# An early first projection and value products paired by heads in a two-layer decoder step

## The reference, cut to what matters

```python
def dilated_group(q, k, v, q_idx, window, dil, table):
    offs = dil * jnp.arange(n_keys, dtype=jnp.int32)
    kg = k[:, idx]; vg = v[:, idx]
    bias = table.astype(jnp.float32)[rel_bucket(offs)].T
    logits = jnp.einsum('bqhd,bqjhd->bqhj', q, kg).astype(jnp.float32) * ATTN_SCALE + bias
    ...
    e = jnp.exp(logits - m)
    s = jnp.sum(e, axis=-1, keepdims=True)
    o = jnp.einsum('bqhj,bqjhd->bqhd', (e / s).astype(v.dtype), vg)
    return o, m + jnp.log(s)

def mixer_a_prompt(h, w_in, w_out, table):
    qkv = (h @ w_in).reshape(bsz, seq, N_DIL, 3, N_HEADS, HEAD_DIM)
```

## Time and profile before

| | us |
|---|---|
| median of 3 runs | 1675.91 |
| lowest and highest | 1675.38, 1677.29 |
| the profiled execution | 1680.73 |
| its span, first to last instruction | 1679.0 |
| TensorE busy | 1579.3 (94% of the span) |
| VectorE busy | 663.4 (40%) |
| ScalarE busy | 387.4 (23%) |
| GpSimd busy | 203.4 (12%) |
| start, to the first projection tile | 56.57 |
| attention A, 382.6 to 507.3 | 124.7 |
| attention B, 1131.2 to 1241.4 | 110.2 |

### The profile page before, as it was taken

How to read it: one execution, slowest core, us unless ns; L and a number is a source line. 1 busy time by engine, 2 the same in 40 slices (tenths; PEclk the granted TensorE clock), 3 DMA queues, 4 the chain that set the end, 5 groups by cost and what they waited for, 6 DMA issues and landing times.

```text
span 1679.0 us, 23479 instructions
## 1 busy us (share of the span) xinstructions
PE 1579.3 (94%) x8609; PEld 1279.6 (76%) x8609; DVE 663.4 (40%) x1533; ACT 387.4 (23%) x1166; POOL 203.4 (12%) x301
## 2 busy tenths in 40 slices
PE   6999998999989999999999999999997778999998
PEld 5877787766878878887888887886764446888886
DVE  2246512118872321003576674326546552322001
ACT  1011111113431000002566663115533220000000
POOL 1100000012230200001111120005532320000000
PEclk8799999999999999999999999999989898999999
DMA  5499999999959998787799991419966877998740
GB/s 183 158 356 383 410 401 360 337 373 355 330 164 249 284 363 299 272 292 135 128 140 140 149 186 38 122 61 352 343 200 220 285 266 242 386 372 304 276 146 31
DMA packets 170979, 423.34 MB, mean 252 GB/s; under 512 B 10400, under 2 KB 131560, under 8 KB 168064
## 3 DMA queue, kind: packets, MB, share of 16 engines
q1 hardware_dynamic: 147840, 344.27, 62.6%
q0 software_dynamic: 19312, 67.47, 15.1%
q10 hardware_dynamic: 3728, 10.32, 1.7%
HBM read 413.88 MB, written 192.48 MB: 361 GB/s over the span
## 4 chain that ended last, share of the span: by engine, by line
PE 82%; DMA 7%; DVE 7%; issue 2%; ACT 1%; SPq 1%; POOL 0%; ACTq 0%; DVEq 0%; POOLq 0%
PE bank L626 21%; PE bank L801 14%; PE bank L787 12%; PE bank L708 4%; PE bank L878 3%; PE bank L881 3%; PE bank L830 3%; PE bank L883 3%; DMA a_win_sample<-oT 2%; PE bank L719 2%; PE bank L663 2%; PE bank L756 1%; DMA cring<-cache_b_kv 1%; PE bank L1041 1%; DMA wring<-mlp_w_up 1%
## 5 line engine op out<-in xcount | busy, mean ns | idle before, releaser
L626 PE MATMUL bank<-hT,wring 128*128 128x264 f32 (+1 forms) x1488 | 354.0, 393 | 0.5 <-DVE area L1359 0.5
L626 PEld LDWEIGHTS bank<-hT,wring 128*128 128x128 f32 (+1 forms) x1488 | 279.2, 192 | 67.2 <-issue 8.2
L787 PE MATMUL bank<-hT,wring 128*128 128x264 f32 x1024 | 230.1, 388 | 1.9 <-DMA wring<-mlp_w_up 1.9
L801 PE MATMUL bank<-area,wring 128*128 128x264 f32 x1024 | 229.2, 386 | 2.8 <-DVE area L1312 2.8
L787 PEld LDWEIGHTS bank<-hT,wring 128*128 128x128 f32 x1024 | 195.6, 191 | 36.1 <-issue 2.3
L801 PEld LDWEIGHTS bank<-area,wring 128*128 128x128 f32 x1024 | 194.1, 190 | 37.2 <-DVE area L1310 3.6
L1689 ACT ACTIVATE turned<-xT 128x264 f32<-128x264 f32 x40 | 16.9, 423 | 548.1 <-DVE xT L1316 463.1
L1316 DVE TENSOR_TENSOR xT<-bank,xT 128x264 f32<-128x264 f32 x16 | 6.9, 432 | 224.6 <-PE bank L801 224.6
L1310 DVE SCALAR_TENSOR_TENSOR area<-bank,rv 128x264 f32 x64 | 27.7, 432 | 163.0 <-PE bank L787 162.3
L567 POOL TENSOR_SCALAR area<-ident,small 128x128 f32<-128x128 f32 x96 | 56.3, 603 | 179.4 <-DVE small L1392 179.4
L1242 DVE TENSOR_TENSOR area<-bank,rv 128x264 f32<-128x264 f32 x48 | 20.8, 432 | 106.0 <-PE bank L626 106.0
(11 more groups left out here) (325 smaller groups left out, 2330.7 us busy)
## 6 DMA issues: line engine op xcount, KB each, us to landing
a_win_sample<-cache_a_win SPq DMA_DIRECT2D x64, 2047.0 KB, 19.5
wring<-a_w_in SPq DMA_DIRECT2D x36, 1024.0 KB, 13.0
wring<-mlp_w_up SPq DMA_DIRECT2D x32, 1024.0 KB, 10.8
wring<-mlp_w_down SPq DMA_DIRECT2D x32, 1024.0 KB, 5.3
a_win_sample<-cache_a_win SPq DMA_DIRECT2D x16, 2044.0 KB, 19.0
cring<-cache_a_win POOLq DMA_DIRECT2D x24, 1024.0 KB, 11.9
cring<-cache_b_kv POOLq DMA_DIRECT2D x62, 256.0 KB, 6.3
cring<-cache_b_kv SPq DMA_DIRECT2D x50, 256.0 KB, 7.7
```

The source lines that it names most:

```text
L626: mm = pe.matmul(bk[half if bank is None else bank][0:width, 0:R], wring[:, blk % NW, c, half * P:half * P + width], rhs[:, c, :], start=( ...
L787: mm = pe.matmul(bk[half][:, 0:R], wring[:, blk % NW, c, half * P:(half + 1) * P], hT[:, c, :], start=(c == 0), stop=(c == DC - 1))
L801: mm = pe.matmul(bk[half][:, 0:R], wring[:, blk % NW, c, half * P:(half + 1) * P], upT[:, f * R:(f + 1) * R], start=(f == 0), stop=(f == F ...
```

## The change

**The start.** The identity is loaded first. TensorE waits for it and for x only, and for the gains ahead of their turning, by a semaphore of their own. Weight block 0 is issued ahead of `c_oh`, the masks and the bias table, which are now loaded into a part of `area` and no longer into `cring`; the first three loads of the old caches on GpSimd's queue wait for the turned gains and no longer for bias products. The bias products are cut into `bias_table(0)` to `bias_table(7)`, which stand behind tiles 1 to 8, and `bias_rest()` behind tile 9; they use banks 5 and 6. VectorE's copies of them stand between its copies of the tiles in the same way.

**Both prompt attentions.** `unit(u)` gives head 2(u // 4) + u % 2 and qt = (u // 2) % 2: two heads of the same half follow each other, so two narrow units are followed by two wide ones. `score_banks(u)` lets the scores go through banks 0, 1, 2 with 0, and 1 with 6. The turned probabilities go to bank 3 or 4, the last blocks of wide units to one half of bank 5, and have four buffers in SBUF. The value products are issued once for two units, the matmuls of the two heads in turn: head 2c writes rows 0 to 63 and head 2c+1 rows 64 to 127 of bank 7. One copy of 128 by 128 takes both out. The mixes of bias and mask have four buffers. The first loads of the compressed keys on SyncE's queue wait for the last value product of attention A, and before for its last logits. The last tiles of layer 1's projection use banks 7 and 5.

```diff
@@ PE @@
-            pe.wait_ge(S["consts_in"], 16 * 13)
+            pe.wait_ge(S["ident_in"], 16)
             pe.wait_ge(S["x_loaded"], 32)
...
+            pe.wait_ge(S["gains_in"], 48)
             pe.transpose(bk[2][:, 0:40], grow_, ident[0:40, 0:40]).then_inc(S["gains_turned"], 1)
...
+                if 1 <= s < 9:
+                    bias_table(s - 1)
+                if s == 9:
+                    bias_rest()
...
@@ units @@
+        def unit(u):
+            return 2 * (u // 4) + u % 2, u // 2 % 2
+        def score_banks(u):
+            return ((bk[0], None), (bk[1], None), (bk[2], bk[0]), (bk[1], bk[6]))[u % 4]
...
@@ PE, attention A @@
-            def pv_a(u):
-                h, qt = u // 2, u % 2
-                pe.wait_ge(S["pt_ready"], u + 1)
-                if u >= 2:
-                    pe.wait_ge(S["o_evac"], u - 1)
-                n, e = qt + 1, h % 2
+            def pv_a(w):
+                c, qt = w // 2, w % 2
+                pe.wait_ge(S["pt_ready"], 2 * w + 2)
+                if w:
+                    pe.wait_ge(S["o_evac"], 2 * w)
+                n = qt + 1
                 for j in range(NG * n):
-                    mm = pe.matmul(bk[6 + u % 2][64 * e:64 * e + 64, 0:P], V[:, j % n, j // n, h * HD:(h + 1) * HD], PT[:, u % 2, j * P:(j + 1) * P],
-                                   start=(j == 0), stop=(j == NG * n - 1))
-                mm.then_inc(S["pv_done"], 1)
+                    for e in range(2):
+                        h = 2 * c + e
+                        mm = pe.matmul(bk[7][64 * e:64 * e + 64, 0:P], V[:, j % n, j // n, h * HD:(h + 1) * HD], PT[2 * qt + e][:, j * P:(j + 1) * P],
+                                       start=(j == 0), stop=(j == NG * n - 1))
+                mm.then_inc(S["pv_done"], 2)
...
-                if u:
-                    pv_a(u - 1)
+                if u and u % 2 == 0:
+                    pv_a(u // 2 - 1)
...
@@ POOL @@
-                if h >= 2:
-                    pool.wait_ge(S["logits_read"], 2 * h - 2)
+                if h in (2, 3):
+                    pool.wait_ge(S["pva_done"], 12)
+                if h >= 4:
+                    pool.wait_ge(S["logits_read"], 4 * (h // 2 - 2) + 3 + h % 2)
...
@@ SP, compressed keys @@
             if b == 0:
-                eng.wait_ge(S["logits_read"], 2 * H)
+                eng.wait_ge(S["pv_done"], 2 * H)
```

More of the change, by code:

```diff
@@ L213, in program @@
         NOH = 2 * 511 + NSL4 * P
-        oh = cring[:, 1, 0:NOH]
-        table = cring[:, 1, NOH:NOH + 4 * H]
-        grow_ = cring[0:40, 1, NOH + 4 * H:NOH + 4 * H + P]
+        oh = at(NOH, NG * DC * R)
+        table = at(4 * H, NG * DC * R + NOH)
+        grow_ = at(P, NG * DC * R + NOH + 4 * H, parts=40)
         xrow = at(RT * D, v_off).rearrange("p (t n) -> p t n", t=RT)
@@ L500, in _ @@
                 sp.dma_start(wring[:, i % NW, :, 0:src.shape[2]], src).then_inc(w_landed[i % NW], 16)
+                if i == 0:
+                    tables()
                 if i < B_AOUT:
@@ L535, in _ @@
             nc.gpsimd.memset(rowv, 0.0).then_inc(S["rows_zero"], 1)
-            a_load(1)
-            a_load(2)
+            for i in range(NA):
+                a_load(i)
             pool.wait_ge(S["bias_evac"], 10)
@@ L595, in _, with bias_table @@
                 sumsq(0, c)
-            for i in range(8):
+            def bias_table(i):
+                if i == 0:
+                    pe.wait_ge(S["consts_in"], 16 * 9)
                 if i >= 2:
@@ L655, in score_a @@
             def score_a(u):
-                h, qt = u // 2, u % 2
+                h, qt = unit(u)
                 q0, c = HD * (h % 2), h // 2
@@ L968, in _ @@
                     score_b(u + 2)
-                n = u % 2 + 1
+                n = unit(u)[1] + 1
                 turn_probs((U0 + u, u), [CMP] + [P] * (2 * n), LB[u % 4], [diag_b[:, u % 2, 0, :]] + [diag_b[:, u % 2, 1, :]] * n + [diag_b[:, u % 2, 2, :]] * n)
-                if u:
-                    pv_b(u - 1)
-            pv_b(2 * H - 1)
+                if u and u % 2 == 0:
+                    pv_b(u // 2 - 1)
+            pv_b(H - 1)
             pe.wait_ge(S["o_evac"], 4 * H)
@@ L1139, in _, with bias_table @@
             norm_rstd(0)
-            for i in range(8):
+            def bias_table(i):
                 dve.wait_ge(S["bias_done"], i + 1)
-                dve.tensor_copy(bias[:, :, 32 * i:32 * i + 32], bk[3 + i % 2].rearrange("p (k h) -> p h k", h=H)).then_inc(S["bias_evac"], 1)
-            dve.wait_ge(S["bias_done"], 9)
-            link(dve.tensor_copy(bias_s[:, :, :], bk[5][:, 0:NSL * H].rearrange("p (s h) -> p s h", h=H)))
-            dve.memset(tabrep.rearrange("p j h -> p (j h)"), 0.0).then_inc(S["tab_ready"], 1)
@@ L1153, in _ @@
-            dve.wait_ge(S["bias_done"], 10)
-            for rt in range(RT):
-                ins = dve.tensor_tensor(bias_c[:, rt, :, :], bk[6][:, rt * CMP * H:(rt + 1) * CMP * H].rearrange("p (n h) -> p h n", h=H),
-                                        mcmp[:, rt, :].unsqueeze(1).broadcast_to([P, H, CMP]), ALU.add)
-            ins.then_inc(S["bias_evac"], 1)
+                dve.tensor_copy(bias[:, :, 32 * i:32 * i + 32], bk[5 + i % 2].rearrange("p (k h) -> p h k", h=H)).then_inc(S["bias_evac"], 1)
@@ L1488, in _ @@
                     max_b(u)
-                if u >= 3:
-                    evac_o(U0, u - 3)
+                if u >= 4 and u % 2 == 0:
+                    evac_o(U0, u // 2 - 2)
                 if u == 4:
@@ L1493, in _ @@
             rc_of(2 * H - 1)
-            for u in range(2 * H - 3, 2 * H):
-                evac_o(U0, u)
+            for w in range(H - 2, H):
+                evac_o(U0, w)
             dve.wait_ge(S["pv_done"], 4 * H)
@@ L1742, in _, with pt_a @@
             ins.then_inc(S["oa_copied"], 1)
-            def copy_pt(u, parts_cols, PTb):
+            def pt_a(u):
+                e = u % 2
+                parts = [(3 + e, 0, 384, 0)] if u // 2 % 2 == 0 else [(3 + e, 0, 512, 0), (5, 256 * e, 256, 512)]
                 act.wait_ge(S["probs_turned"], u + 1)
-                if u >= 2:
-                    act.wait_ge(S["pv_done"], u - 1)
-                for parts, bank, c0, n, o in parts_cols:
-                    ins = nc.scalar.copy(PTb[0:parts, o:o + n], bk[bank][0:parts, c0:c0 + n])
+                if u >= 4:
+                    act.wait_ge(S["pv_done"], 2 * (u // 2 - 1))
+                for bank, c0, n, o in parts:
+                    ins = nc.scalar.copy(PT[u % 4][:, o:o + n], bk[bank][:, c0:c0 + n])
                 ins.then_inc(S["pt_ready"], 1)
-            def pt_a(u):
-                copy_pt(u, [(P, 3, 0, 384, 0)] if u % 2 == 0 else [(P, 4, 0, 512, 0), (P, 5, 0, 256, 512)], PT[:, u % 2, :])
             for u in range(2 * H):
```

200 lines of the change are left out of this document (110 added, 90 removed).

## The result

The changed kernel took 1704.53 us in the median of four runs (1696.17 to 1713.28), against 1675.64 (1667.56 to 1677.29) for the kernel before beside it: a ratio of 1.018, 95% interval 1.012 to 1.024. I had forecast 1663. The profiled execution took 1713.28, span 1711.6.

What follows compares the result with a forecast made beforehand. TensorE, busy 94% of the span, was taken as the bound. Profiled 1680.7 - 20.3 (start) + 2 (attention A) + 5 (attention B) = 1667.4, less 4.8 to the median: 1663 us, range 1645 to 1687.

Steps and rivals of the forecast that it cites:

- The start: Up to tile 10: TensorE starts at 7.0, first tile at 20.2, tile 10 at 75.1 instead of 95.4; -20.3 us.
- The bias products: Between the first tiles: full clock, groups of 16 instructions at 0.115 us plus 0.15 per bank change, 15.9 for eight groups.
- Attention A: Paired values save 4.2 us at full clock, four clock falls cost 6; together +2, bounds -5 and +12.
- the chain that I had summed: Attention A: VectorE's 7.4 us plus TensorE's 6.4 us set a round of 13.8, against 14.18 before.
- both collisions: Attention A: two VectorE diagonals per round last 1.93 us beside GpSimd's mix, where one takes 0.35 alone.
- the gap ahead of the first wide turning: Attention A: TensorE stands still about 1.9 us a round, most of it in one piece there.
- B at full clock: Attention B: TensorE stands 1.5 us once in four units; a round of 13.2 against 13.96, -5 over eight rounds.
- a fall in most rounds, at 1.5 or, where it holds on, a little more: +10: Attention B: the recurring gap drops the clock in most rounds, costing 10 us, so B together is +5.
- (b): Attentions: gaps keep B at 1.2 GHz mostly, B +18 to +28, A +6 to +12; 1680 to 1695 us; chance 0.18.
- (a): Attentions: the clock doesn't fall in the new gaps, A -4, B -5; 1646 or 1647 us; chance 0.18.
- (c): Attentions: paired products don't run side by side, A +7, B +12; 1674 or 1675 us; chance 0.08.
- (d): Start: bias products run at half clock, +14, 1677 us; chance 0.06.

Runs made afterwards that it cites:

- start alone: Kernel before with only the new start, both attentions untouched: 1649.67, 1695.09, 1696.14 and 1704.87 us.
- start and A: Kernel before with the new start and paired values in attention A, attention B untouched: 1657.48, 1698.19, 1730.78 and 1732.78 us.
- the fills in B: Changed kernel with unused matmuls in attention B, six at the second turning, three at each unit with u % 4 = 2: 1653.33 to 1665.80 us, ratio 0.989.
- A unpaired: Kernel before with the new start, GpSimd's bias operation behind attention A, unused matmuls at attention B's entry: nine runs 1648.50 to 1669.79 us, one 1722.82.
- late mixes: Changed kernel with GpSimd's two mixes of each attention A round begun behind the next round's narrow logits: 1679.58 to 1698.61 us.

## Why the prediction was wrong

**What held.** The start: TensorE at 7.80 (7.0), first tile at 20.05 (20.2), tile 10 at 73.05 (75.1): -22.3 for -20.3. The bias products ran at clock 1.00, 1.73 us for a group and not 1.99, which is the 2 us. Attention A: +1.6 for +2. The round at full clock was 13.5 (13.8), by the chain that I had summed, with both collisions; the pairs ran side by side; the gap ahead of the first wide turning was 1.73 at full clock and 2.05 to 2.25 in the first three rounds (1.9 a round). That the sum fits is luck: the clock fell in the first four rounds, for 6.8 to 10.2 us each, and the second to fourth took 17.2 to 17.9 and not 13.5, so a fall cost 3.6 to 4.4 where I took 1.5. It fits because the kernel before has long rounds too, the second and third with 17.3 us and falls of their own, where I reckoned with 14.18 throughout. B at full clock: gap 1.47 (1.5), round 13.29 (13.2).

**The step that failed** is the price of the falls in B: "a fall in most rounds, at 1.5 or, where it holds on, a little more: +10". There was one fall, at the entry, and it lasted to the end: +49.3 in place of +5. That is rival (b), to which I gave 0.18. The wait in front of the fall, 2.62 us at the third unit, stands in no term of my sum, which knew the gaps of the rounds alone. The price of (b) was wrong too. I took 17 to 18 us for a round at half clock, because gaps would be filled (that is 24 to 32 us in all, and not the 18 to 28 that I wrote). But with 20.75 us of work at half clock there is no gap left to fill; my own 11.4 doubled was 22.8, and the reason to lower it to 18 didn't hold. Eight rounds of 20.75 - 13.96 are 54, the measured +49. With that price (b) would have stood at 1676 - 20 + 2 + 54 = 1712 even with the forecast's +2 for A, above my range.

**What I should have read.** I took the recovery in A as the rule for B. The earlier trace rows showed the other case: 24 us at 0.51 with TensorE busy, through short products, ended only by tiles of 264 columns. And B's entry in the kernel before has a wait of 1.03 us, which the timeline shows and I passed over:

```profile
1136.47 1.02 PE L708 MATMUL bank<-area,turned 128*15 128x128 f32 x6 [1.03 <-POOL area L567]
```

That kernel was at the edge itself: in 24 of its 58 runs it took some 43 us more, on average. Falls in B's order of before made it 52 us (start alone) and 76 us (start and A) longer than the 107.6 of before. That this is B is inferred from the lower mean clock of those 24 (0.92 to 0.95 against 0.96 to 0.97) and from the trace of the start alone, 1704.87 us with B in the order of before; none of the 24 was traced itself. Three runs that were all among the short ones told me nothing of it. What the change did to B is to turn a fall that comes in part of the runs into one that came in all.

**The rivals.** (a), no falls, didn't happen; the fills in B brought it about there for all but one round, and the time to 1659, where (a), with A's falls gone too, said 1646. (c), pairs not side by side, fell: 24 instructions in 1.53 us. The rule of the Trainium skill ("TensorE: Matmul & The Clock Gate", "Part 3: Packing small matmuls — row/col tiling") that loads overlap only where row groups differ doesn't forecast this case: both heads use all 128 rows. The table "Measured speedup vs the span model" of the same page of the Trainium skill gives three products packed by columns, 32 each, 2.38 times the speed. The trace agrees with a gain of that kind, two products in the time of one, if the groups take turns from one matmul to the next (1.53 us, against 2.46 one after the other). (d), bias products at half clock, fell.

## What to carry to other kernels

A gap in TensorE's work has to be priced by what stands behind it: if that is a long stretch of short products, one gap of 1 to 3 us can make the whole stretch half as long again or more (rounds of 20.75 for 13.29, 24.83 for 13.94). Here it paid more to fill the gaps with useless dense matmuls (45 us) than to shorten the work around them (5 us in B at full clock). When an engine off the bound (here GpSimd's mix against VectorE's diagonal) sits in the new chain, move it to where its collision hits slack before judging the change. And time a kernel that is near such an edge often enough to see both of its times.

## What the runs showed of the hardware

- The clock can stay at its lower level with TensorE busy: 118.0 of 118 us (start alone) and 175.0 of 175 (start and A), both at 0.50. It came back behind a piece of six matmuls of 128 by 256 in one trace, and behind one of three in another. In others it came back with no such piece, after 20 (A unpaired), 34 (late mixes) and 119 us (start alone).
- The same program is short or long from run to run (start alone: 1649.67 and 1704.87). The clock fell behind waits of 0.76, 1.04, 1.47, 1.51 and 2.62 us, and held through waits of 0.75 and 1.03 (before), 1.47 and 1.48 (late mixes) and 1.73 (changed kernel, attention A). So the length of the wait alone doesn't tell.
- VectorE's diagonal of 0.35 us ends with GpSimd's operation beside it: it took 1.93 with a mix of 1.80, and 6.77 where it began 2.2 us behind the start of the 8.85 us on the bias (changed kernel).
- Matmuls of alternating column halves, 64 result rows each, cost one for two (24 instructions in 1.53 us, where 12 of one half take 1.52); one half after the other the 24 take 2.46.
